# Attention mask of a hybrid DiT kernel: added by VectorE to the scores in PSUM instead of by TensorE products

## What is computed

```
def window_attention(u, uc, w_qkv, sink, w_o, cos, sin, need_ctx_out):
    ...
    rel = jnp.arange(span)[None, :] - jnp.arange(A_BLOCK)[:, None]
    band = (rel >= 0) & (rel <= 2 * A_WINDOW)
    def block(bi):
        ...
        valid = band & ((kpos >= 0) & (kpos < n))[None, :]
        s_loc = jnp.where(valid, jnp.einsum('bqkgd,bskd->bkgqs', qb, kb).astype(jnp.float32), -jnp.inf)
        s_ctx = jnp.einsum('bqkgd,bskd->bkgqs', qb, kc).astype(jnp.float32)
        p = jax.nn.softmax(jnp.concatenate([s_loc, s_ctx, s_snk], -1), axis=-1).astype(u.dtype)
        return (jnp.einsum('bkgqs,bskd->bqkgd', p[..., :span], vb)
                + jnp.einsum('bkgqs,bskd->bqkgd', p[..., span:span + n_ctx], vc))
```

## Time and profile before

| | us |
|---|---|
| median of three runs | 2747.99 |
| the profiled execution, its own time | 2748.45 |
| its span in the profile | 2746.6 |
| TensorE busy (94%) | 2590.3 |
| VectorE busy (44%) | 1214.4 |
| ScalarE busy (31%) | 837.7 |
| GpSimd busy (58%) | 1603.8 |

### The profile page before, as it was taken

How to read it: one execution, slowest core, us unless ns; L and a number is a source line. 1 busy time by engine, 2 the same in 40 slices (tenths; PEclk the granted TensorE clock), 3 DMA queues, 4 the chain that set the end, 5 groups by cost and what they waited for, 6 DMA issues and landing times. The chain is left out here.

```text
span 2746.6 us, 45735 instructions
## 1 busy us (share of the span) xinstructions
PE 2590.3 (94%) x16441; PEld 2099.7 (76%) x16441; DVE 1214.4 (44%) x2266; ACT 837.7 (31%) x1603; POOL 1603.8 (58%) x1625
## 2 busy tenths in 40 slices
PE   6999999999899799999999989898999999898998
PEld 4767677788688689767778858896677788677997
DVE  2363522222569677451222230486522222655555
ACT  2263312211541444141121133252322211354542
POOL 2545566676557222556667656785566667655664
PEclk8999999999999899999999999999999999999999
DMA  7343455423123000255542222101455422212553
GB/s 249 115 147 123 160 177 181 143 96 100 54 72 93 31 2 2 77 171 166 183 152 93 92 65 77 47 1 62 154 168 183 163 90 98 81 44 78 180 173 107
DMA packets 217164, 305.62 MB, mean 111 GB/s; under 512 B 7331, under 2 KB 155550, under 8 KB 217023
## 3 DMA queue, kind: packets, MB, share of 16 engines
q1 hardware_dynamic: 179007, 228.16, 25.2%
q10 hardware_dynamic: 38016, 75.50, 8.4%
HBM read 302.60 MB, written 1.05 MB: 111 GB/s over the span
## 5 line engine op out<-in xcount | busy, mean ns | idle before, releaser
L611 POOL TENSOR_TENSOR w_lo<-w_raw,w_hi 128x512 fp32r<-128x512 f32 x676 | 893.0, 1321 | 98.8 <-POOL w_hi L608 77.8
L608 POOL TENSOR_SCALAR w_hi<-w_raw 128x512 fp32r<-128x512 f32 x676 | 440.1, 651 | 737.2 <-PE bank L1162 455.5
L1162 PE MATMUL bank<-u_lo,w_hi 128*128 128x512 f32 (+1 forms) x2144 | 812.4, 379 | 35.8 <-DVE u_lo L1913 30.6
L1162 PE MATMUL bank<-u_hi,w_lo 128*128 128x512 f32 (+1 forms) x2144 | 795.7, 371 | 0.0
L1162 PE MATMUL bank<-u_hi,w_hi 128*128 128x512 f32 (+1 forms) x2144 | 795.2, 371 | 0.0
L1162 PEld LDWEIGHTS bank<-u_lo,w_hi 128*128 128x128 f32 x2144 | 411.0, 192 | 173.3 <-issue 89.0
L1162 PEld LDWEIGHTS bank<-u_hi,w_hi 128*128 128x128 f32 x2144 | 411.2, 192 | 68.9
L1162 PEld LDWEIGHTS bank<-u_hi,w_lo 128*128 128x128 f32 x2144 | 412.1, 192 | 63.3
L2575 DVE SCALAR_TENSOR_TENSOR cv<-bank,vec,cv 128x510 f32<-128x510 f32 (+1 forms) x88 | 59.6, 677 | 347.9 <-ACT cv L1082 347.9
L1802 PE MATMUL bank<-gs_lo,w_hi 128*128 128x512 f32 (+1 forms) x576 | 209.4, 364 | 1.8 <-POOL w_lo L611 1.8
L1802 PE MATMUL bank<-gs_hi,w_lo 128*128 128x512 f32 (+1 forms) x576 | 209.1, 363 | 0.0
(11 more groups left out here) (349 smaller groups left out, 3883.9 us busy)
## 6 DMA issues: line engine op xcount, KB each, us to landing
w_raw<-in_ffn_w_up SPq DMA_DIRECT2D x88, 1024.0 KB, 7.2
ada_w<-in_ada_w ACTq DMA_DIRECT2D x72, 1024.0 KB, 5.2
w_raw<-in_ffn_w_down SPq DMA_DIRECT2D x44, 1024.0 KB, 4.9
ada_w<-in_ada_w SPq DMA_DIRECT2D x16, 1024.0 KB, 5.1
w_raw<-in_gdn_w_in SPq DMA_DIRECT2D x16, 1024.0 KB, 5.7
w_raw<-in_attn_w_qkv SPq DMA_DIRECT2D x12, 1024.0 KB, 5.1
w_raw<-in_gla_w_in SPq DMA_DIRECT2D x12, 1024.0 KB, 5.3
ada<-in_ada_w SPq DMA_DIRECT2D x8, 1024.0 KB, 13.7
```

The costliest lines, as they stand in the source:

```text
L608: eng.tensor_scalar(w_hi[:, q, :], src, 1.0, 0.0, ALU.mult, ALU.add).then_inc(pool.own, pool.step())
L611: eng.tensor_tensor(w_lo[:, q, :], src, w_hi[:, q, :].bitcast(F32), ALU.subtract).then_inc(w_split, 1)
L1162: mm = eng.matmul(bank[banks[m]][:, T], w[:, q, c:c + P], v[:, k, T], start=(k == 0 and n == 0), stop=(k == KT - 1 and n == 2))
```

## The change

The mask products leave TensorE's program. The scores' products now all end their own sum (`stop=True`), and the last of them raises `score_ready`. In VectorE's program, for pairs with qt of 2 or 3, a `tensor_tensor` addition comes first: it adds the mask, repeated for both heads, to the block of 128 columns in the two banks, in place in PSUM. VectorE waits for its end and then takes the maximum as before. The mask's numbers in `con` stay as they are.

```diff
--- before.py
+++ after.py
@@ -1228,12 +1228,7 @@
                             for m in range(2):
                                 r = 64 * m
                                 mm = eng.matmul(bank[2 * (i % 2) + m][:, c:c + 256], aq[r:r + 64, t, qt * P:(qt + 1) * P],
-                                                akd[r:r + 64, t // 2, c:c + 256], start=True, stop=(qt < 2 or c == 0))
-                        if qt >= 2:
-                            c = 384 if qt == 2 else 256
-                            for m in range(2):
-                                mm = eng.matmul(bank[2 * (i % 2) + m][:, c:c + P], ident, con[:, K_AM + (qt - 2) * P:K_AM + (qt - 1) * P],
-                                                start=False, stop=True)
+                                                akd[r:r + 64, t // 2, c:c + 256], start=True, stop=True)
                         mm.then_inc(score_ready, 1)
                     if i - 3 == len(pairs):
                         eng.wait_ge(pts_ready, pe.next(pts_ready, 2))
@@ -1984,6 +1979,12 @@
                         t, qt = pairs[i]
                         mx, nm, es = (ast[:, k, i % 4, :] for k in (0, 1, 2))
                         eng.wait_ge(score_ready, dve.next(score_ready))
+                        if qt >= 2:
+                            c = 384 if qt == 2 else 256
+                            block = banks[:, 2 * (i % 2):2 * (i % 2) + 2, c:c + P]
+                            mask = con[:, K_AM + (qt - 2) * P:K_AM + (qt - 1) * P].unsqueeze(1).to_broadcast([P, 2, P])
+                            eng.tensor_tensor(block, block, mask, ALU.add).then_inc(dve.own, dve.step())
+                            eng.wait_ge(dve.own, dve.count())
                         eng.tensor_reduce(mx, banks[:, 2 * (i % 2):2 * (i % 2) + 2, 0:keys(qt) * P], AX.X, ALU.max).then_inc(dve.own, dve.step())
                         eng.wait_ge(dve.own, dve.count())
                         eng.scalar_tensor_tensor(nm, mx, -A_SCALE, nsink[:, slot, 2 * t:2 * t + 2], ALU.mult, ALU.min).then_inc(dve.own, dve.step())
```

## The result

The changed kernel takes 2733.62 us (median of 5 runs, 2728.67 to 2735.74) against 2747.99 us (5 runs, 2745.71 to 2750.35): ratio 0.9947, 95% interval 0.9934 to 0.9961, so -14.4 us. Forecast were -9.2 us and 2739.0, with a range down to 2734.5. The profiled execution took 2728.67 us (span 2726.9, mean granted clock 0.979), the shortest of its five; the one before took 2748.45 (2746.6, 0.977).

The account below looks back on a forecast made before the run. TensorE was taken to bound both cores, with VectorE setting layer 3's pace after the change. Layer 0's -6.3 us and layer 3's -2.9 sum to -9.2, giving 2739.0 us, range 2734.5 to 2746.5.

Parts of the forecast that it names:

- the first two rounds of layer 0: Start of layer 0's core: exponentials govern, so these rounds gain only 1.0 us together.
- Price of a product: Both cores: removing the mask products saves 0.49 us of TensorE's time for each masked pair.
- the level chain: Layer 0, masked pair of qt 2: VectorE's copies end at 4.75 us, TensorE asks at 4.72; longer additions cost one to one.
- Price of an addition: VectorE, both cores: each mask addition in PSUM delays the maximum by 0.46 us, bounds 0.35 to 0.94.
- Rival (a): Reading and writing one PSUM bank goes at half pace, 0.73 us an addition: 2745 us; chance 0.14.
- Layer 3 (-2.9 us, VectorE sets the pace at 6.35): Layer 3's core: VectorE's 6.35 us a round of two exceeds TensorE's 6.07, so the core gains 2.9 us.
- Rival (c): VectorE has room after all, so about 13 us of the 15.7 show: 2735 us; chance 0.05.
- a fixed tail: End of layer 3's core: scale on GpSimd, transposes, copies and value products behind the last pair keep their length.
- rival (d): TensorE's clock falls after longer waits in layer 3: some 8 us slower (2756), up to 37 (2785); chance 0.06.
- Layer 0 (-6.3 us: Layer 0's core: TensorE stays the bound; five steady rounds give 4.7 us, first two 1.0, last 0.6.
- Around it: Outside the two cores: nothing moves, and no loss at the output product is counted; 0 us.
- Rival (b): The gain is given back at the output product or in a later stage: 2748 us; chance 0.07.

Follow-up runs that it names:

- second profile: The changed kernel run again with no edit: 2733.82 us, ratio 0.9961 to the kernel before; cores 109.80 us in layer 0 and 59.56 in layer 3.
- e1_l0_only: Kernel before with VectorE's mask addition in layer 0 alone, layer 3 keeping the mask products: 2734.93 us, ratio 0.9964.
- e2_l3_only: Kernel before with VectorE's mask addition in layer 3 alone, layer 0 keeping the mask products: 2739.91 us, ratio 0.9991.
- e3_no_mask: Changed kernel with the mask left out, neither products nor additions: 2726.01 us, ratio 0.9939 to the kernel before.
- e5_both: Kernel before with VectorE's addition put in and the mask products kept: 2747.2 us, ratio 1.0004.
- e10_fill: Kernel with both moves plus unused products in TensorE's waits at the start of layer 3's core: 2726.59 us, ratio 0.9934 to the kernel before.
- e7_before_copy: Word for word copy of the kernel before, run against it: 2745.97 us, ratio 1.0002.
- e9_both_moves: Changed kernel; layer 3's rounded copy moved to ScalarE, layer 0's output copies made before VectorE's wait for scores: 2728.68 us, ratio 0.9939 to the kernel before.
- e11_moves_again: The changed kernel with both moves, run once more without further edit: 2728.78 us, ratio 0.9944 to the kernel before.

## Why the prediction was right in most steps and short in its sum

Two terms of the sum failed: the first two rounds of layer 0 (1.0 us in the sum, 1.9 measured), and what stands around the cores (nothing in the sum and half a us of scatter in the range; 4 us measured, some 3 of them in the runs of before). The second put the measurement out of the range.

**Price of a product (0.49 us of TensorE): right.** The masked pair lost 2.14 - 1.69 = 0.45 us in layer 0, and layer 3 without mask ran the worked-out 6.07 us. Layer 0's round lost 0.94 to 0.95 us; without mask and additions it is 13.11 us, so the additions cost it 0.04, about what the level chain (4.75 against 4.72) had said.

**Price of an addition (0.46 us): right.** 0.46 us in the steady part, 426 ns of it the instruction. Rival (a), the half pace in PSUM at 0.73 us, is refuted by 32 records between 422 and 433 ns. The Trainium skill's rule (SBUF — State Buffer, Who interferes with whom) fits: one SBUF input, GpSimd at work, and no second level of durations.

**Layer 3 (-2.9 us, VectorE sets the pace at 6.35): right, with luck.** 6.36 us and -3.0 in the first profile. Rival (c), room on VectorE, is refuted: taking the additions away, or the copy off VectorE, gives 6.07. The second profile gave -1.4, by TensorE's low clock at the core's end, where I had written a fixed tail and the wait for GpSimd grew from 0.67 to 1.93 us. This and the spell at the start are rival (d) in a small form: 1.6 and 0.15 us in place of 8.

**Layer 0 (-6.3 us): the term of the first two rounds was too small.** Distances of maxima, before and after: first round 10.68 and 9.75, second 13.96 and 13.01, then five of 14.09 and 13.15, the last part 21.11 and 20.49. The five steady rounds gave 4.7 and the last part 0.6, both as predicted. The first two gave 1.9, not 1.0. I had put them down to the exponentials, where a pair gains only 0.18 us, but the second round at 13.96 us was already within 1% of the steady one and so TensorE's; the trace of before held that number. In the first round TensorE's only waits are the 1.89 us before the first masked pair, the same in both kernels, and one near its end, first of before, then of the changed kernel:

```profile
136.04 0.70 PE L1230 MATMUL bank<-akd,aq 64*128 64x256 f32 x4 [0.63 <-ACT ap L810]
```

```profile
124.40 1.13 PE L1230 MATMUL bank<-akd,aq 64*128 64x256 f32 x8 [1.89 <-ACT ap L810]
...
132.79 0.70 PE L1230 MATMUL bank<-akd,aq 64*128 64x256 f32 x4 [0.80 <-ACT ap L810]
```

The exponentials took 0.80 - 0.63 = 0.17 us of the gain there and no more. A spell of the low clock lies in this round in both kernels; its share was not separated. Layer 0: -7.2 us, seen in all three profiles with this core (109.72, 109.80, 109.91).

**Around it (no loss, no gain): the step that put the measurement out of the range.** The cores give -10.2 us, at 2737.8 from the median shown, inside the range. The other 4 us of -14.4 have two parts. First, the runs of before beside which the change was first measured were high: 2747.99, where 47 later runs of the same kernel have a median of 2744.93. With the later ones, the changed kernel's ten runs (median 2733.71) are at -11.2 us. So some 3 us of the 4 are a high group of runs of before. Why it was high stays open: it is more than the scatter of the 47 gives a median of five, and the three later groups ran on three chips, the chip of the first being unknown; the share of the chips no run separates. Second, the whole time follows the granted clock: those 47 runs average 2746.05 us at a clock of 0.976 (9 runs), 2745.72 at 0.977 (15), 2744.84 at 0.978 (11), 2743.34 at 0.979 (6) and 2741.33 at 0.98 (5). The correlation is -0.74, and 0.001 of clock is worth 1.2 us. Which spells at the low level an execution gets differs with no code changed. I gave that "half a us of scatter" in the range; the 47 runs spread over 9.5 us, and medians of five drawn from them scatter by about 1 us, while the medians of the three groups differ by 2. Had I written 2 us, the range would have begun at 2733.

**What stays open.** At one clock, 0.977, the changed kernel's five runs average 2732.96 and the kernel before's 15 average 2745.72: -12.8 us, where the two profiles' cores give -10.2 and -8.5. The same sign stands in `e1_l0_only`, `e2_l3_only`, `e3_no_mask` and `e5_both` (2.0 to 3.4 us less in the whole than in the cores) and in `e10_fill` (1.8); `e7_before_copy` shows none, nor do `e9_both_moves` and `e11_moves_again` (0.5 us at most). Only `e5_both`'s is outside its interval. Whether an addition or a shorter core shifts later spells in a helpful way was not separated: between the cores the second profile of the changed kernel is 3.6 us shorter than either profile of before, with as long at the low level as the first of them (85.3 us) and less than the second (92.2). Rival (b), a gain given back later, is refuted all the same: nothing was given back.

**The clock.** In layer 3's core every one of the seven profiles with additions or without products and without filling fell to the low level near the start: five after waits of 2.88 and 0.86 us, `e3_no_mask` after one of 2.42, `e5_both` after one of 2.04. The three with products and no additions there never did, after waits of 1.57 and 0.70 us; the two filled ones, with no wait over 0.96 us inside the core, didn't either. `e3_no_mask` has no additions, so VectorE's work in PSUM isn't the cause. The length of a wait doesn't decide it alone, though: at this core's end 1.93 us came before a fall in one profile of the changed kernel and before none in the other. The Trainium skill (TensorE: Matmul & The Clock Gate, HAM oscillation — how this bites in real kernels) says that idle gaps throttle the engine, and the runs agree that it happens. What a spell costs depends on the place: 0.15 us or little more at this core's start, where TensorE waits anyway, and 1.6 us at its end.

**The better version.** `e9_both_moves` and `e11_moves_again` have a median of 2728.68 us over 9 runs, ratios 0.9939 and 0.9944; `e10_fill` has 0.9934, with an interval that overlaps theirs. The changed kernel's ten runs have a median of 2733.71 us (0.9947 and 0.9961). By the medians the two moves give another 5 us, as expected, but on different chips, and the intervals of the ratios overlap; what is clear is that the cores are 4.8 to 7.7 us shorter, at rounds of 12.51 and 6.07 us for 13.15 and 6.36. What the filling adds to that can't be told from none.

## What to carry to other kernels

Work moved from the bound engine to one with idle time is worth its full price only until the second engine's own round is reached: add up both rounds before, here 6.07 against 6.35 us, and the smaller gain is the answer. It also names the next edit: take work off the new bound, here a copy of 0.42 us. Price a start-up round by its measured length, not by its name: a round within 1% of the steady one is steady. And before a range of 0.1% is written, look at how the same program's runs spread and whether that goes with the granted clock.

## What the runs showed of the hardware

- VectorE adds in place in PSUM at the price of an addition into SBUF: 426 against 424 ns for 256 f32 elements with one PSUM input.
- The same eight score records take 1.13 or 2.08 us. At the start of layer 3's core they took 2.08 behind waits of 2.88 and 0.86 us, and products put into those waits removed the fall in 2 profiles of 2. At the core's end the same wait of 1.93 us came before a fall in one profile and before none in another.
- Two executions of one program differed by 8.85 us (2719.13 and 2727.98), at mean granted clocks of 0.979 and 0.977; 8.2 us of it lie between the cores, with 75.1 and 85.3 us at the low level there.
